# The begin of an eight-layer block on one NeuronCore: smaller first transfers, x and the first products taken piece by piece, and spare products ahead of both

## The chip, the cores and the metric

The kernel runs on one core of one Trainium2 chip. It is one launch that computes a whole eight-layer block for 256 tokens. The metric is the device time of that core in microseconds, lowest is best. Three runs of the kernel before took 2028.44, 2028.63 and 2031.82 us; their median, 2028.63 us, is the time before.

## The reference, cut to what matters

`x` has 256 tokens of 1024 features. Eight layers follow one another, each reading and adding to `x`: differential attention, a conformer convolution, latent attention, differential attention again, a window attention with a convolution, a gated feed-forward, a recurrent mixer and a mixture of eight experts. The change touches only what is computed first, the norm and the first projection of layer one:

```
def _rms_norm(x, g):
    xf = x.astype(jnp.float32)
    y = xf * lax.rsqrt(jnp.mean(xf * xf, axis=-1, keepdims=True) + NORM_EPS)
    return (y * g.astype(jnp.float32)).astype(x.dtype)

h = _rms_norm(x, a_norm_g[j])                       # (256, 1024)
proj = h @ w_in                                     # (1024, 4096): q, k, v, gate
q, k, v, gate = jnp.split(proj, [A_QK_WIDTH, 2 * A_QK_WIDTH, 2 * A_QK_WIDTH + A_WIDTH], axis=-1)
```

All later layers are computed by the same code in both kernels.

## The kernel before, in words

Tokens lie in two tiles of 128 partitions (`TILES`), features in eight chunks of 128 (`KC`). For a product TensorE needs the features on the partitions, so `norm_tensor` first turns `x`: 16 transposes of 128x128 (L1371), four to a PSUM bank, `("norm", 0, i)` for i from 0 to 3; each bank holds two chunks for both tiles. ScalarE (`high_parts`, L1105) and then VectorE (`low_parts`, L1117) read a bank, multiply by the norm's gain, which lies in the `vecs` part of the constants, and write `hT.high` and `hT.low`: every number is kept as two fp32r parts. `low_parts` frees the bank. The root of the mean square is left for later.

Weights come as granules of 128x2048 numbers (1 MB). A granule holds four chunks of 512 columns. The raw granule is split too: ScalarE writes `high`, VectorE writes `low` = raw - high. From the third granule on this is one instruction on each engine for a whole granule (L986, L989, called by `ahead`, which splits as many granules as there is room for before a given step). The first two are split in quarters of 128x512, one chunk each, by `split_first_piece` (L1000 on ScalarE, L1006 on VectorE). A product of one chunk is three matmuls of 512 columns (`three_passes`, L1022 to L1024): high by high, high by low, low by high. `products` takes granule 0, then granule 1: in each it goes through the four chunks for token tile 0 and then through the same four chunks for token tile 1. A granule is thus 2 x 4 x 3 = 24 matmuls.

SyncE issues every load, in the order of `sync_weights`: `x` tile 0, `x` tile 1, the first constants (`ident`, the identity that the transposes need, 16 columns for roots, and `vecs`: 656 columns, 328 KB), granule 0, the other constants (512 KB), `spread` (388 KB), granules 1 to 3, the lambdas and the router, then granules 4 and 5; from the seventh on a load waits until its buffer has been split. The constants have one semaphore, `const_landed`, for which TensorE, ScalarE, VectorE and GpSimd wait.

The order of the work on ScalarE at the begin is: load an activation table, the squares of tile 0, `hT.high` of banks 0 and 1, four quarters of granule 0, `hT.high` of banks 2 and 3, four quarters of granule 1, granule 2. VectorE does the same with the low parts; between granules 1 and 2 it computes twelve small tables for the rotation (`rope_tables`, L1046 to L1048).

Of the kernel before, what the change touches and what calls it, by code (L numbers as in the profile page):

```python
# [32 lines left out]
F32 = mybir.dt.float32  # L33
# [5 lines left out]
P = 128  # L39
# [635 lines left out]
class Core:  # L675


    def __init__(self, nc, ctx, w, consts, const_at, out, banks, plan):
# [40 lines left out]
        self.back, self.count, self.neghalf = const("back"), const("count"), const("neghalf")  # L719
        self.vecs = const("vecs").rearrange("p (c r) -> p c r", c=KC)  # L720
        self.first_const = const_at["cos"][0]


        at = 0
# [36 lines left out]

        self.x_landed = [sem(f"x_landed_{t}") for t in range(TILES)]
        self.const_landed = sem("const_landed")
        self.rest_landed = sem("rest_landed")
        self.spread_landed = sem("spread_landed")
        self.lambdas_landed = sem("lambdas_landed")
# [162 lines left out]

def sync_weights(k, sp):  # L930

    for t in range(TILES):
        sp.dma_start(k.x[:, t, :], k.w["x"][0].rearrange("(t p) d -> p t d", p=P)[:, t, :]).then_inc(k.x_landed[t], 16)
    sp.dma_start(k.const[:, 0:k.first_const], k.consts[:, 0:k.first_const]).then_inc(k.const_landed, 16)
    for g, granule in enumerate(k.granules):
        if g == 1:
            sp.dma_start(k.const[:, k.first_const:], k.consts[:, k.first_const:]).then_inc(k.rest_landed, 16)
            sp.dma_start(k.spread[:, :], k.w["spread"][:, 0:N_SPREAD].broadcast_to([P, N_SPREAD])).then_inc(k.spread_landed, 16)
        if g == 4:
            last_loads(k, sp)  # L940
        if g >= RAW:

            before = k.granules[g - RAW]
            if before.plain:
                k.wait_used(sp, before.last)
            else:
                sp.wait_ge(k.low_ready, before.number + 1)
        c, n = granule.shape
        sp.dma_start(k.raw[:, g % RAW, 0:c * n], k.w["weights"][g][:, 0:c * n]).then_inc(k.landed[g % RAW], 16)


def ahead(k, eng, name, limit=None):
# [36 lines left out]
        eng.tensor_tensor(low, raw, high.bitcast(F32), ALU.subtract).then_inc(k.low_ready, 1)  # L989


def split_first_piece(k, eng, g):

    n = GRANULE // 4
    if eng is k.nc.scalar:
        k.wait_landed(eng, g)
    for c in range(4):
# [16 lines left out]
def granule_parts(k, g, c):  # L1014

    n, slot = k.granules[g].shape[1], k.granules[g].number % SPLIT
    parts = Parts(k.high[:, slot, 0:c * n], k.low[:, slot, 0:c * n])
    return parts.rearrange("p (c n) -> p c n", c=c)


def three_passes(pe, out, lhs, rhs, start, stop):
# [226 lines left out]
def norm_scalar(k, act, n, x_from):  # L1248
    if n in RAW_NORMS:
        half_squares(k, act, x_from[0][0], 1)  # L1250
        high_parts(k, act, n, (2, 3))
        if n not in UNSCALED:
            act.wait_ge(k.rstd_ready, untiled(n) + 1)
            act.activation(k.h[:, 0, :], k.x[:, 0, :], ACT.Copy, scale=k.rstd[:, 0:1]).then_inc(k.h_ready, 1)
        ahead(k, act, ("norm", n, 3))
        return
    if n == 0:
        act.wait_ge(k.x_landed[0], 16)
        act.activation(k.h[:, 0, :], k.x[:, 0, :], ACT.Square, scale=float(D) ** -0.5, accum_out=k.ms[:, 0:1]).then_inc(k.ms_ready, 1)
        act.wait_ge(k.const_landed, 16)  # L1260
        high_parts(k, act, n, (0, 1))
        split_first_piece(k, act, 0)
        high_parts(k, act, n, (2, 3))
        split_first_piece(k, act, 1)
        ahead(k, act, ("norm", n, 3))
        return
    tiled_scalar(k, act, n, x_from)
    gain = NORM_GAIN[n]
    for i in range(4):
        name = ("norm", n, i)  # L1270
        if n == 1 and i % 2 == 0:
# [12 lines left out]

def norm_vector(k, v, n, x_from):
    if n in RAW_NORMS:
# [5 lines left out]
        ahead(k, v, ("norm", n, 3))  # L1292
        return
    if n == 0:
        v.wait_ge(k.x_landed[1], 16)
        v.tensor_tensor_reduce(k.h[:, 1, :], k.x[:, 1, :], k.x[:, 1, :], 1.0 / D, 0.0, ALU.mult, ALU.add, k.ms[:, 1:2])\
         .then_inc(k.ms_ready, 1)
        v.wait_ge(k.const_landed, 16)
        low_parts(k, v, n, (0, 1))
        split_first_piece(k, v, 0)  # L1300
        low_parts(k, v, n, (2, 3))
        split_first_piece(k, v, 1)
        b = a_buffers(k, 0)
# [5 lines left out]
        ahead(k, v, ("norm", n, 3))  # L1309
        return  # L1310
    tiled_vector(k, v, n, x_from)
    gain = NORM_GAIN[n]
# [42 lines left out]
def norm_tensor(k, pe, n):  # L1355
    k.normed, k.to_turn = (n, 0), None
    if n in RAW_NORMS:
        k.to_turn = n
        return
    if n in TILED:  # L1360
        tiled_tensor(k, pe, n)
        return
    pe.wait_ge(k.const_landed, 16)
    for t in range(TILES):
        pe.wait_ge(k.x_landed[t], 16)
    for i in range(4):
        k.take(pe, ("norm", n, i))
        for c in (2 * i, 2 * i + 1):
            for t in range(TILES):
                first = SEQ * (c % 2) + P * t  # L1370
                last = pe.transpose(k.bank(("norm", n, i))[:, first:first + P], k.x[:, t, P * c:P * (c + 1)], k.ident)  # L1371
        k.fill(last, ("norm", n, i))

def wait_normed(k, pe, parts):

# [8 lines left out]
def products(k, pe, names, g, lhs, kc, n, first=0, halves=2, ready=None, turn=None):  # L1384

    for half in range(halves):
        if g + half > 1:
            wait_split(k, pe, g + half)
        chunks = kc // halves
# [22 lines left out]
        if half < halves - 1:  # L1412
            last.then_inc(k.half_done, 1)
            if turn is not None:
                turn_x(k, pe, turn, (0, 1))


def channel_product(k, pe, name, g):
# [2312 lines left out]
def build(nc, w, consts, const_at, out, banks, plan, layers=LAYERS):  # L3731
    with ExitStack() as ctx:
# [44 lines left out]
        def _(pool):  # L3777
            k.engine_steps["pool"] = Steps(pool, k.own["pool"])
            for n, layer in enumerate(layers):
                if n == 0:  # L3780
                    for first, end, value in ((0, CHUNK, MASKED), (CHUNK, P, 0.0), (P, 2 * P, 1.0)):
                        pool.memset(k.late_keys[0:1, first:end].bitcast(F32), value).then_inc(k.late_keys_ready, 1)
                    pool.wait_ge(k.const_landed, 16)
                norm_pool(k, pool, n)
                if layer[0] == "a":
                    a_pool(k, pool, int(layer[1]))
# [73 lines left out]
```

## Time and profile before

| | us |
|---|---|
| median of three runs | 2028.63 |
| lowest and highest | 2028.44, 2031.82 |
| span of the profiled execution | 2030.7 |
| TensorE busy in it | 1940.3 |
| VectorE busy | 1566.0 |
| ScalarE busy | 1241.0 |
| GpSimd busy | 160.4 |

The profile is of one execution. Its span, from the first to the last instruction, is 2030.7 us; it gives no other time of its own, and this span is 2.1 us above the median of the runs shown and within their spread. All positions are microseconds from the start of the span. The 40 slices of the page show TensorE at nine tenths or more in 32 of them; the first slice, 51 us long, is at eight. The same page gives a mean of 249 GB/s for the DMA engines; the first slice has 330 GB/s.

### The profile page before, as it was taken

The numbers are of one execution on the slowest core, as the hardware profiler recorded it, in microseconds if no ns is written. First come the engines' busy times: TensorE is split into PE (matmuls) and PEld (weight loads), VectorE is DVE, ScalarE is ACT, GpSimd is POOL, SyncE is SP. The second block draws the span as 40 slices with busy tenths as digits, with TensorE's granted clock in tenths as the row PEclk, the third lists the DMA queues.
The fourth block names the chain that finished last, engine by engine and source line by source line (L and its number), as shares of the span: only waits on it lengthen the run. The fifth ranks groups of instructions, "written<-read, shape, count | busy, mean of one in ns | idle before, by whom it ended". The sixth has DMA issues, their size and how long they took to land.

```text
span 2030.7 us, 26201 instructions
## 1 busy us (share of the span) xinstructions
PE 1940.3 (96%) x9320; PEld 1619.0 (80%) x9320; DVE 1566.0 (77%) x1881; ACT 1241.0 (61%) x1461; POOL 160.4 (8%) x228
## 2 busy tenths in 40 slices
PE   8989988899989899999999999999999999999998
PEld 6867877778778788888878878888888888888886
DVE  7765966867656654446878898989889898998987
ACT  5562145645654544344767767777777777777775
POOL 4113401313011000000000000000000000000000
PEclk9999999999989999999999999999999999999999
DMA  8422234324324255553459999899999989999994
GB/s 330 157 84 104 93 125 140 125 104 180 113 82 178 92 207 187 187 187 125 187 229 382 355 353 376 343 382 351 372 375 349 376 342 385 353 373 374 341 376 174
DMA packets 71802, 504.78 MB, mean 249 GB/s; under 512 B 8864, under 2 KB 8864, under 8 KB 11808
## 3 DMA queue, kind: packets, MB, share of 16 engines
q1 hardware_dynamic: 70432, 498.87, 64.8%
q0 software_dynamic: 1280, 4.72, 0.6%
q8 instruction: 55, 0.90, 0.2%
q14 instruction: 35, 0.29, 0.0%
HBM read 501.46 MB, written 2.10 MB: 248 GB/s over the span
## 4 chain that ended last, share of the span: by engine, by line
PE 84%; DVE 8%; ACT 5%; issue 2%; POOL 1%; DMA 0%; DVEq 0%; SPq 0%; ACTq 0%; POOLq 0%
PE psum L1022 24%; PE psum L1024 24%; PE psum L1023 24%; PE psum L1958 4%; DVE low L989 3%; ACT high L986 2%; PE psum L3486 1%; PE psum L1966 1%; ACT h L1694 1%; PE psum L3417 0%; PE psum L1974 0%; DVE small L1738 0%; PE psum L1566 0%; DMA const<-in_constants 0%; PE psum L1143 0%
## 5 line engine op out<-in xcount | busy, mean ns | idle before, releaser
L989 DVE TENSOR_TENSOR low<-raw,high 128x2048 fp32r<-128x2048 f32 x459 | 1044.9, 2281 | 265.5 <-ACT high L986 261.9
L986 ACT ACTIVATE high<-raw 128x2048 fp32r<-128x2048 f32 x459 | 876.9, 1912 | 371.3 <-PE psum L1024 352.6
L1022 PE MATMUL psum<-high,yT_high 128*128 128x512 f32 (+1 forms) x1672 | 664.6, 397 | 25.9 <-DVE yT_low L3695 6.5
L1024 PE MATMUL psum<-high,yT_low 128*128 128x512 f32 (+1 forms) x1672 | 653.3, 391 | 0.0
L1023 PE MATMUL psum<-low,yT_high 128*128 128x512 f32 (+1 forms) x1672 | 652.1, 390 | 0.0
L1022 PEld LDWEIGHTS psum<-high,yT_high 128*128 128x128 f32 x1672 | 315.5, 189 | 95.6 <-issue 14.2
L1024 PEld LDWEIGHTS psum<-high,yT_low 128*128 128x128 f32 x1672 | 315.3, 189 | 67.1
L1023 PEld LDWEIGHTS psum<-low,yT_high 128*128 128x128 f32 x1672 | 316.0, 189 | 61.0
L1022 PE MATMUL psum<-high,hT_high 128*128 128x512 f32 (+2 forms) x560 | 220.8, 394 | 1.6 <-DVE low L1006 0.9
L1024 PE MATMUL psum<-high,hT_low 128*128 128x512 f32 (+2 forms) x560 | 217.3, 388 | 0.0
L1023 PE MATMUL psum<-low,hT_high 128*128 128x512 f32 (+2 forms) x560 | 217.3, 388 | 0.0
L1022 PEld LDWEIGHTS psum<-high,hT_high 128*128 128x128 f32 x560 | 106.0, 189 | 23.6 <-issue 1.8
L1024 PEld LDWEIGHTS psum<-high,hT_low 128*128 128x128 f32 x560 | 105.9, 189 | 21.5
L1023 PEld LDWEIGHTS psum<-low,hT_high 128*128 128x128 f32 x560 | 106.2, 190 | 20.1
L1958 PE MATMUL psum<-arena,raw 128*128 128x256 f32 x384 | 84.5, 381 | 0.0
L1958 PEld LDWEIGHTS psum<-arena,raw 128*128 128x128 f32 x384 | 73.4, 191 | 10.3 <-issue 0.2
L2065 DVE SCALAR_TENSOR_TENSOR arena<-arena,const 128x256 f32<-128x256 f32 x184 | 74.3, 480 | 0.4
L1022 PE MATMUL psum<-hT_high,high 128*128 128x256 f32 x224 | 66.9, 299 | 3.6 <-DVE hT_low L1325 2.4
L3343 POOL DMA_INDIRECT arena<-rows,index x7 | 8.7, 1242 | 765.1 <-DVE index L3692 765.1
L1023 PE MATMUL psum<-hT_low,high 128*128 128x256 f32 x224 | 65.8, 294 | 0.0
L1024 PE MATMUL psum<-hT_high,low 128*128 128x256 f32 x224 | 65.6, 293 | 0.0
L3550 ACT ACTIVATE arena<-psum 128x512 f32<-128x512 f32 x56 | 33.6, 599 | 45.6 <-PE psum L1024 45.6
(367 smaller groups left out, 1714.9 us busy)
## 6 DMA issues: line engine op xcount, KB each, us to landing
raw<-in_moe_weights SPq DMA_DIRECT2D x336, 1024.0 KB, 4.9
raw<-in_weights SPq DMA_DIRECT2D x132, 1024.0 KB, 4.9
raw<-in_weights SPq DMA_DIRECT2D x2, 896.0 KB, 4.7
raw<-in_weights SPq DMA_DIRECT2D x2, 768.0 KB, 8.1
x<-in_x SPq DMA_DIRECT2D x2, 512.0 KB, 3.9
raw<-in_weights SPq DMA_DIRECT2D x2, 512.0 KB, 3.6
rows<-h POOLq DMA_DIRECT2D x1, 1024.0 KB, 4.8
out_x<-x SPq DMA_DIRECT2D x1, 1024.0 KB, 5.5
```

The costliest lines, as they stand in the source:

```text
L986: eng.activation(high, raw, ACT.Copy).then_inc(k.high_ready, 1)
L989: eng.tensor_tensor(low, raw, high.bitcast(F32), ALU.subtract).then_inc(k.low_ready, 1)
L1022: pe.matmul(out, lhs.high, rhs.high, start=start, stop=False)
L1023: pe.matmul(out, lhs.high, rhs.low, start=False, stop=False)
L1024: return pe.matmul(out, lhs.low, rhs.high, start=False, stop=stop)
L1694: last = act.activation(probs[:, s % 2, SEQ * m:SEQ * m + e], k.bank(name)[:, SEQ * m:SEQ * m + e], ACT.Exp, bias=low[:, m:m + 1], scale=q ...
L1958: last = pe.matmul(k.bank(name)[:, SEQ * half:SEQ * (half + 1)], w[:, c, P * half:P * (half + 1)], b.hT[:, c, :], start=(c == 0), stop=(c ...
L1966: last = pe.matmul(k.bank(name)[:, SEQ * half:SEQ * (half + 1)], b.diagonals[i % 2][:, half, tap, :], b.padded[:, 2 * i + half, tap:tap + ...
L2065: last = v.scalar_tensor_tensor(b.conv[:, c, :], window, weight, b.conv[:, c, :], ALU.mult, ALU.add)
L3343: pool.indirect_dma_start(b.rows, None, rows, bass.IndirectOffsetOnAxis(ap=k.index[:, 0:1], axis=0)).then_inc(k.gathered, 16)
L3486: last = pe.transpose(k.bank(name)[:, P * c:P * (c + 1)], b.hidden[:, i % 2, P * c:P * (c + 1)], k.ident)
L3550: k.release(act.activation(b.silu[:, i % 2, :], k.bank(name), ACT.Silu), name)
```

## The change

The identity and 16 columns (144 columns, 72 KB) are loaded first, alone. Tile 1 of `x` follows on SyncE's queue; tile 0 is issued by ScalarE as its first instruction. `vecs` (256 KB) comes next with a semaphore of its own, then granule 0 as four transfers of 256 KB, one to a quarter, each with its semaphore. The other constants and `spread` move from ahead of granule 1 to behind granule 2. TensorE turns all of tile 0 and then all of tile 1. ScalarE and VectorE do one bank, two quarters, the next bank, two quarters. The products of granule 0 go chunk by chunk, both tiles in each, with both PSUM banks taken ahead. Twelve products of ones by ones (256 columns) are put ahead of the transposes and four ahead of the first real product; VectorE fills the ones first. The rotation tables move behind the split of granule 2.

```
+    sp.dma_start(k.const[:, 0:k.first_vecs], k.consts[:, 0:k.first_vecs]).then_inc(k.const_landed, 16)
+    load_x(k, sp, 1)
+    sp.dma_start(k.const[:, k.first_vecs:k.first_const], k.consts[:, k.first_vecs:k.first_const]).then_inc(k.vecs_landed, 16)
     for g, granule in enumerate(k.granules):
-        if g == 1:
+        if g == 0:
+            n = GRANULE // 4
+            for c in range(4):
+                cols = slice(n * c, n * (c + 1))
+                sp.dma_start(k.raw[:, 0, cols], k.w["weights"][0][:, cols]).then_inc(k.quarter_landed[c] if c < 3 else k.landed[0], 16)
+            continue
+        if g == 3:
             sp.dma_start(k.const[:, k.first_const:], k.consts[:, k.first_const:]).then_inc(k.rest_landed, 16)
             sp.dma_start(k.spread[:, :], k.w["spread"][:, 0:N_SPREAD].broadcast_to([P, N_SPREAD])).then_inc(k.spread_landed, 16)
...
+def load_x(k, eng, t):
+    eng.dma_start(k.x[:, t, :], k.w["x"][0].rearrange("(t p) d -> p t d", p=P)[:, t, :]).then_inc(k.x_landed[t], 16)
...
+def spare_products(k, pe, bank, n):
+    ones = k.yT.high[:, 0, :]
+    for _ in range(n):
+        pe.matmul(bank[:, 0:SEQ], ones[:, 0:P], ones, start=True, stop=True)
...
     if n == 0:                                     # norm_scalar
+        load_x(k, act, 0)
         act.wait_ge(k.x_landed[0], 16)
...
-        act.wait_ge(k.const_landed, 16)
-        high_parts(k, act, n, (0, 1))
-        split_first_piece(k, act, 0)
+        act.wait_ge(k.vecs_landed, 16)
+        for part in range(2):
+            high_parts(k, act, n, (part,))
+            split_first_piece(k, act, 0, (2 * part, 2 * part + 1))
...
+    pe.wait_ge(k.spare_ready, 1)                   # norm_tensor
+    k.take(pe, ("norm", n, 0))
+    spare_products(k, pe, k.bank(("norm", n, 0)), 12)
     pe.wait_ge(k.const_landed, 16)
     for t in range(TILES):
         pe.wait_ge(k.x_landed[t], 16)
-    for i in range(4):
-        k.take(pe, ("norm", n, i))
-        for c in (2 * i, 2 * i + 1):
-            for t in range(TILES):
+        for i in range(4):
+            if t == 0:
+                k.take(pe, ("norm", n, i))
+            for c in (2 * i, 2 * i + 1):
...
+def first_products(k, pe, names, lhs):
+    w = granule_parts(k, 0, 4)
+    for name in names:
+        k.take(pe, name)
+    spare_products(k, pe, k.bank(names[0]), 4)
+    for c in range(4):
+        wait_normed(k, pe, c // 2 + 1)
+        if c < 3:
+            pe.wait_ge(k.first_low, c + 1)
+        else:
+            wait_split(k, pe, 0)
+        for t, name in enumerate(names):
+            last = three_passes(pe, k.bank(name), lhs[:, c, P * t:P * (t + 1)], w[:, c, :], c == 0, False)
+    last.then_inc(k.half_done, 1)
```

`norm_vector` changes in the same way as `norm_scalar`, and its `ahead(k, v, ("norm", n, 3))` moves ahead of the two calls of `rope_tables`. GpSimd waits for `vecs_landed` as well.

TensorE at the begin of the program, before; `freed_0` and `freed_1` count how often VectorE has released PSUM banks 0 and 1, and `first_low` counts the low quarters:

```order
L1371 MATMUL psum<-const,x 128x128 [waits x_landed_1,x_landed_0,const_landed]
L1371 MATMUL psum<-const,x 128x128 x15
L1022 MATMUL psum<-high,hT_high 128x512 [waits first_low,freed_0]
L1023 MATMUL psum<-low,hT_high 128x512
L1024 MATMUL psum<-high,hT_low 128x512
L1022 MATMUL psum<-high,hT_high 128x512 [waits first_low]
```

And of the change:

```order
L1042 MATMUL psum<-yT_high 128x256 [waits spare_ready]
L1042 MATMUL psum<-yT_high 128x256 x11
L1402 MATMUL psum<-const,x 128x128 [waits x_landed_0,const_landed]
L1402 MATMUL psum<-const,x 128x128 x7
L1402 MATMUL psum<-const,x 128x128 [waits x_landed_1]
L1402 MATMUL psum<-const,x 128x128 x7
L1042 MATMUL psum<-yT_high 128x256 [waits freed_1,freed_0]
L1042 MATMUL psum<-yT_high 128x256 x3
L1046 MATMUL psum<-high,hT_high 128x512 [waits first_low,freed_0]
```

The transposes no longer wait for all of the constants, and half of them wait for one tile of `x` only; the four spare products ahead of the first real one wait for the release of bank 1 as well as bank 0.

VectorE up to the split of granule 1, before:

```order
L1296 ISA h,small<-x 128x1024 [waits x_landed_1]
L1296 ISA small 128x1
L1117 SCALAR_TENSOR_TENSOR hT_low<-psum,const,hT_high 128x256 [waits part_ready,const_landed]
L1117 SCALAR_TENSOR_TENSOR hT_low<-psum,const,hT_high 128x256
L1117 SCALAR_TENSOR_TENSOR hT_low<-psum,const,hT_high 128x256 [waits part_ready]
L1117 SCALAR_TENSOR_TENSOR hT_low<-psum,const,hT_high 128x256
L1006 TENSOR_TENSOR low<-raw,high 128x512 [waits first_high] x3
L1006 TENSOR_TENSOR low<-raw,high 128x512 [waits high_ready]
```

And of the change:

```order
L1321 MEMSET yT_high 128x256
L1323 ISA h,small<-x 128x1024 [waits x_landed_1]
L1323 ISA small 128x1
L1141 SCALAR_TENSOR_TENSOR hT_low<-psum,const,hT_high 128x256 [waits part_ready,vecs_landed]
L1141 SCALAR_TENSOR_TENSOR hT_low<-psum,const,hT_high 128x256
L1023 TENSOR_TENSOR low<-raw,high 128x512 [waits first_high] x2
L1141 SCALAR_TENSOR_TENSOR hT_low<-psum,const,hT_high 128x256 [waits part_ready]
L1141 SCALAR_TENSOR_TENSOR hT_low<-psum,const,hT_high 128x256
L1023 TENSOR_TENSOR low<-raw,high 128x512 [waits first_high]
L1023 TENSOR_TENSOR low<-raw,high 128x512 [waits high_ready]
```

Two quarters of granule 0 now stand ahead of the second pair of `hT_low`, whose last instruction is the one that releases bank 1.

SyncE's loads up to the fourth granule, of the change:

```order
L936 DMA const<-in_constants 128x144
L963 DMA x<-in_x 128x1024
L938 DMA const<-in_constants 128x512
L944 DMA raw<-in_weights 128x512 x4
L959 DMA raw<-in_weights 128x2048 x2
L947 DMA const<-in_constants 128x1024
L948 DMA spread<-in_spread 128x776
L959 DMA raw<-in_weights 128x2048
```

The loads ahead of the last quarter of granule 0 are of the same total size as those ahead of the end of granule 0 before; the two 512 KB and 388 KB loads stand two granules later.

## Rows read from the trace of the kernel before

**Rows 1.** The page's fourth part, shares of the chain that ended last.

```profile
PE 84%; DVE 8%; ACT 5%; issue 2%; POOL 1%; DMA 0%; DVEq 0%; SPq 0%; ACTq 0%; POOLq 0%
```

**Rows 2.** Chain of waits to 20 us, its longest pieces: start, us, what.

```profile
1.64 6.81 DMA const<-in_constants
8.49 1.13 PE psum L1371 x4
9.71 0.85 ACT hT_high L1105 x2
10.68 1.66 DVE hT_low L1117 x4
12.34 0.61 DVE low L1006
```

**Rows 3.** Stretch: us, PE, PEld, DVE, ACT, POOL busy, PEclk, DMA share, GB/s.

```profile
20.00:60.00 40.00, 40.00 (x187) 33.27 (x186) 34.47 (x50) 22.73 (x23) 17.75 (x12) 1.00 0.67 264
```

**Rows 4.** Timeline of TensorE: start, us, line, tile, [idle before].

```profile
8.49 3.68 PE L1371 MATMUL psum<-const,x 128*128 128x128 f32 x16 [8.49 <-DMA const<-in_constants]
13.08 0.77 PE L1022 MATMUL psum<-high,hT_high 128*128 128x512 f32 x1 [0.91 <-DVE low L1006]
...
17.48 0.45 PE L1023 MATMUL psum<-low,hT_high 128*128 128x512 f32 x1
17.77 0.40 PE L1024 MATMUL psum<-high,hT_low 128*128 128x512 f32 x1
18.00 0.40 PE L1022 MATMUL psum<-high,hT_high 128*128 128x512 f32 x1
```

**Rows 5.** Busy time by stretch of the begin, with the DMA columns.

```profile
1.70:5.50 3.80, 0.00 (x0) 0.00 (x0) 0.00 (x0) 1.45 (x3) 0.00 (x0) 1.00 0.95 317
5.50:8.50 3.00, 0.01 (x1) 0.01 (x1) 1.23 (x2) 0.00 (x0) 0.00 (x0) 1.00 1.03 359
8.50:13.00 4.50, 3.67 (x16) 3.27 (x16) 2.32 (x6) 3.29 (x8) 2.20 (x5) 1.00 1.01 362
```

**Rows 6.** Tile x up to 3 us: its two loads.

```profile
DMA to landing us min/median/max: 3.5/3.9/4.3
```

**Rows 7.** DMA packets from 6.6 to 8.0 us.

```profile
DMA packets 58, 0.48 MB, mean 339 GB/s; under 512 B 0, under 2 KB 0, under 8 KB 0
```

**Rows 8.** Timeline of ScalarE.

```profile
0.71 1.28 ACT L1259 ACT_TABLE_LOAD   x1 [0.71 <-PEq L3835]
...
9.71 1.63 ACT L1105 ACTIVATE hT_high<-psum,const 128x256 fp32r<-128x256 f32 x4 [4.31 <-PE psum L1371]
11.23 2.18 ACT L1000 ACTIVATE high<-raw 128x512 fp32r<-128x512 f32 x4
...
21.67 1.92 ACT L986 ACTIVATE high<-raw 128x2048 fp32r<-128x2048 f32 x1 [0.75 <-DMA raw<-in_weights]
```

**Rows 9.** Timeline of VectorE.

```profile
12.25 2.49 DVE L1006 TENSOR_TENSOR low<-raw,high 128x512 fp32r<-128x512 f32 x4
...
23.70 2.29 DVE L989 TENSOR_TENSOR low<-raw,high 128x2048 fp32r<-128x2048 f32 x1 [0.44 <-ACT high L986]
25.90 0.68 DVE L1852 TENSOR_TENSOR h<-psum,h 128x512 f32<-128x512 f32 x1
```

**Rows 10.** VectorE's groups by shape: a memset of 128x512.

```profile
L2370 DVE MEMSET arena<- 128x512 f32 x1 | 0.5, 485 | 0.1
```

**Rows 11.** Timeline of TensorE near 291 us.

```profile
290.82 0.77 PE L1022 MATMUL psum<-high,yT_high 128*128 128x512 f32 x1 [4.87 <-DVE yT_low L2108]
...
293.94 0.46 PE L1023 MATMUL psum<-low,yT_high 128*128 128x512 f32 x1
```

**Rows 12.** Busy time by stretch around it.

```profile
290.70:294.10 3.40, 3.28 (x8) 2.63 (x9) 1.74 (x5) 2.23 (x6) 0.00 (x0) 0.50 0.00 0
```

**Rows 13.** Timeline of TensorE near 596 us: products of 256 columns.

```profile
596.33 0.41 PE L1024 MATMUL psum<-hT_high,low 128*128 128x256 f32 x1
596.54 0.41 PE L1022 MATMUL psum<-hT_high,high 128*128 128x256 f32 x1
```

More of the change, by code:

```diff
@@ L721, in __init__ @@
         self.first_const = const_at["cos"][0]
+        self.first_vecs = const_at["vecs"][0]
         at = 0
@@ L763, in __init__ @@
         self.const_landed = sem("const_landed")
+        self.vecs_landed = sem("vecs_landed")
+        self.quarter_landed = [sem(f"quarter_landed_{i}") for i in range(3)]
+        self.spare_ready = sem("spare_ready")
         self.rest_landed = sem("rest_landed")
@@ L930, in sync_weights @@
 def sync_weights(k, sp):
-    for t in range(TILES):
-        sp.dma_start(k.x[:, t, :], k.w["x"][0].rearrange("(t p) d -> p t d", p=P)[:, t, :]).then_inc(k.x_landed[t], 16)
-    sp.dma_start(k.const[:, 0:k.first_const], k.consts[:, 0:k.first_const]).then_inc(k.const_landed, 16)
+    sp.dma_start(k.const[:, 0:k.first_vecs], k.consts[:, 0:k.first_vecs]).then_inc(k.const_landed, 16)
+    load_x(k, sp, 1)
+    sp.dma_start(k.const[:, k.first_vecs:k.first_const], k.consts[:, k.first_vecs:k.first_const]).then_inc(k.vecs_landed, 16)
     for g, granule in enumerate(k.granules):
-        if g == 1:
+        if g == 0:
[5 more added lines that the diff above has]
+        if g == 3:
             sp.dma_start(k.const[:, k.first_const:], k.consts[:, k.first_const:]).then_inc(k.rest_landed, 16)
@@ L989, in split, with split_first_piece @@
         eng.tensor_tensor(low, raw, high.bitcast(F32), ALU.subtract).then_inc(k.low_ready, 1)
-def split_first_piece(k, eng, g):
+def split_first_piece(k, eng, g, quarters=range(4)):
     n = GRANULE // 4
-    if eng is k.nc.scalar:
-        k.wait_landed(eng, g)
-    for c in range(4):
+    for c in quarters:
+        if eng is k.nc.scalar:
+            if g == 0 and c < 3:
+                eng.wait_ge(k.quarter_landed[c], 16)
+            elif g == 0 or c == 0:
+                k.wait_landed(eng, g)
         high, low, raw = (a[:, g, n * c:n * (c + 1)] for a in (k.high, k.low, k.raw))
@@ L1294, in norm_vector @@
     if n == 0:
+        v.memset(k.yT.high[:, 0, :].bitcast(F32), 1.0).then_inc(k.spare_ready, 1)
         v.wait_ge(k.x_landed[1], 16)
@@ L1297, in norm_vector @@
          .then_inc(k.ms_ready, 1)
-        v.wait_ge(k.const_landed, 16)
-        low_parts(k, v, n, (0, 1))
-        split_first_piece(k, v, 0)
+        v.wait_ge(k.vecs_landed, 16)
+        for part in range(2):
+            low_parts(k, v, n, (part,))
+            split_first_piece(k, v, 0, (2 * part, 2 * part + 1))
         low_parts(k, v, n, (2, 3))
         split_first_piece(k, v, 1)
+        ahead(k, v, ("norm", n, 3))
         b = a_buffers(k, 0)
@@ L1308, in norm_vector @@
         rope_tables(k, v, None, b.k_tables, k.wide("a_k_norm_g", 0, A_QK))
-        ahead(k, v, ("norm", n, 3))
         return
@@ L1365, in norm_tensor @@
         pe.wait_ge(k.x_landed[t], 16)
-    for i in range(4):
-        k.take(pe, ("norm", n, i))
-        for c in (2 * i, 2 * i + 1):
-            for t in range(TILES):
+        for i in range(4):
+            if t == 0:
+                k.take(pe, ("norm", n, i))
+            for c in (2 * i, 2 * i + 1):
                 first = SEQ * (c % 2) + P * t
                 last = pe.transpose(k.bank(("norm", n, i))[:, first:first + P], k.x[:, t, P * c:P * (c + 1)], k.ident)
-        k.fill(last, ("norm", n, i))
+            if t == 1:
+                k.fill(last, ("norm", n, i))
 def wait_normed(k, pe, parts):
@@ L1386, in products @@
     for half in range(halves):
+        if g + half == 0:
+            first_products(k, pe, names, lhs)
+            continue
         if g + half > 1:
@@ L3783, in _ @@
                     pool.wait_ge(k.const_landed, 16)
+                    pool.wait_ge(k.vecs_landed, 16)
                 norm_pool(k, pool, n)
```

## The prediction

> **What bounds the kernel now.** I read the shares of the chain first. TensorE has 84% of it and DMA rounds to 0% [rows 1]: what the begin takes from TensorE is all that this change can give. The chain in order of time then shows who holds the begin [rows 2]: the first constants are in flight from 1.64 to 8.45, then follow four transposes, two `hT_high` on ScalarE, four `hT_low` on VectorE, the first `low` quarter, and the first real product starts at 13.08 [rows 4]. The reader is to see that each link waits for the one ahead, so that a microsecond taken from the transfer is one taken from the first product, until something else comes last. Next I looked whether a gain would last. From 20 to 60 us TensorE is busy for 40.00 of 40.00 us while VectorE has 34.47 and ScalarE 22.73 [rows 3]: TensorE is the bound there and the two others have room, so an earlier start moves all later work with it.
>
> The timeline of TensorE shows a second cost. From 13.08 to 17.48 the products start 10 in 4.40 us, 0.43 each after the first; from 17.77 to 18.00 it is 0.23 [rows 4]. The clock column says 1.00 for this stretch [rows 5], but 0.43 is the spacing of a stretch whose granted clock is 0.50 (eight products in 3.4 us, [rows 11, 12]). So TensorE begins at its lower level of 1.2 GHz and goes to 2.4 GHz after 4.4 us of products. That costs 10 x 0.2 = 2.0 us.
>
> **The transfers.** In MB to a landing: identity 0.07, x 1.05, `vecs` 0.26, together 1.39; x with all first constants was the same 1.39. The engines are at 0.95 to 1.03 of their time and move 317 GB/s up to 5.5 us, then 359 and 362 [rows 5]; they are the limit, and the change removes no byte ahead of the end of granule 0. Tile 0 of x landed 3.5 us after its issue at 0.71, at 4.2, tile 1 at about 5.5 (4.3 after 1.17) [rows 6]. With the identity ahead and both tiles under way together I put tile 0 at 4.3 to 5.0 and tile 1 at 5.5 + 0.07/0.36 = 5.7. `vecs` would by bytes end 0.26/0.36 = 0.7 later, at 6.4. But before, the same 1.39 MB had landed only at 8.45, and no packet under 8 KB (the constants' are 2.6 KB) started between 6.6 and 8.0 [rows 7]: all but the last packets were through by about 6.9 and one late one held the landing. Without that `vecs` is there by 6.9, with it at 8.5. I take 6.9, nearer to the packet rows, and keep 8.5 as an end. The quarters follow at 0.73 us each: 7.6, 8.3, 9.0, 9.8; granule 1 is 2.9 later, 12.7, granule 2 at 15.6.
>
> The row says that the sixteen engines were already full with one queue. The Trainium skill says in "DMA: Bandwidth & Descriptors", section "Issuing engines are not separate DMA queues", that loads issued by several engines run on the same 16 DMA engines and only the issue time is saved; the trace agrees in its 0.95 share. If the second queue doubled the rate, both tiles would be there at 3.7 and the first product another 0.6 us earlier.
>
> **The first product, step by step.** The ones (128x256) take VectorE half of 485 ns [rows 10] from 0.7 on. Twelve spare products at 0.21 (the spacing of 256 columns at the lower level, [rows 13]) run from 1.1 to 3.7, ahead of tile 0: cost 0. They would cost if x came at 3.7 or before. ScalarE's issue (0.4) and its table load (1.28, [rows 8]) end at 2.4, also under the transfer. Transposes are 3.68/16 = 0.23 apart [rows 4]: tile 0 from 4.3 to 6.15, tile 1 from the later of that and 5.7, so bank 0 is filled with the second transpose of tile 1, at 6.15 + 2 x 0.23 and about 0.3 of latency, 6.9. That is when `vecs` is there; ScalarE starts at 7.0.
>
> ScalarE: `hT_high` is 1.63/4 = 0.41, a quarter 2.18/4 = 0.55 [rows 8]. Bank 0 done at 7.85, quarters 0 and 1 at 8.95, bank 1 at 9.8, quarters 2 and 3 at 10.9. VectorE: `hT_low` 0.41 [rows 2], a low quarter 2.49/4 = 0.62 [rows 9]. It starts 0.1 behind ScalarE, as at 10.68 before: bank 0 from 8.0 to 8.8, quarters 0 and 1 to 10.05, bank 1 to 10.9, quarters 2 and 3 to 12.15.
>
> Now the wait that the change adds. The four spare products need bank 0 and bank 1, and behind them stands every real product. Bank 1 is released at 10.9, though bank 0 and quarter 0 are ready at 9.4. So 1.5 us of the quicker first chunk are not used. The spare ones run from 11.0 to 11.85 (4 x 0.21), and the first real product starts at 11.85, against 13.08: 1.23 us. The chunk order then asks for a quarter every six products (2.6 us) where before it was every three; quarters 2 and 3 at 11.5 and 12.15 are in time. The halves of granule 1 are low from about 14.5 to 16.5, wanted at 19.
>
> The clock: TensorE is busy without a gap from 11.0. It rose 4.4 us after the first product in one place and 3.1 us (290.82 to 293.94, after 4.87 idle, [rows 11]) in the other. I take 4.4: it rises at 15.4. Real products at the lower level are (15.4 - 11.85)/0.43 = 8.3 in place of 10.3, a gain of 2 x 0.2 = 0.4. With 3.1 it is 5.3 of them, a gain of 1.0. That the transposes or the twelve spare ones help is not in the sum: before, 16 transposes in a row from 8.49 to 12.17 did not spare the products 4.4 us of the lower level. The Trainium skill says the same in "TensorE: Matmul & The Clock Gate", "Part 4: PE-mode transpose": such transposes don't count as TensorE being busy for its clock. By that rule the gap between 3.7 and 11.0 is idle to the gate and the twelve are lost; the sum goes by this. If transposes counted, the clock would be up by 11, which is the first rival.
>
> **Later effects, each at nothing.** The other constants and `spread` now follow granule 2: 15.6 + 0.92/0.36 = 18.2. The tables come after the low part of granule 2 (about 18 to 20.3), so at 20.3 to 21.7; their first user ran at 25.90, behind granule 3's low part (23.70 + 2.29, [rows 9]), which hangs on the landing of granule 3 at 21.67 [rows 8]. Bytes ahead of that are the same, so this user does not come earlier, nor later. TensorE needs granule 3 at about 30 and the freed bank 0 after that: cover of 4 us. If it is gone, each us late costs one. GpSimd's wait for `vecs` ends earlier than its wait for the constants did.
>
> Sum: 1.23 + 0.4 = 1.6 us less. The profiled span of 2030.7 would be 2029.1. That span is 2.1 above the median; the difference is taken off both sides, so 2028.6 - 1.6 = 2027.0.
>
> **The rivals.**
>
> A. The clock is up at the first real product. For it: twelve spare ones, 16 transposes and four spare ones are 2.6 + 3.7 + 0.9 us of work in the ten ahead. Against: the idle time between, and the 4.4 us after the transposes before. Then the four spare ones take 0.45, the first product starts at 11.45, and none is slow: 1.63 + 10.3 x 0.2 = 3.7 less, 2024.9. Chance 0.15.
>
> B. The late packet comes again, in `vecs`. Everything behind moves by 1.5: first product at 13.35, 0.27 later than before; the clock, counted from the spare ones at 12.5, rises at 16.9 and 8.3 products are slow: 0.4 back. Result 0.1 less, 2028.5. Chance 0.2.
>
> C. Slower: more stretches at half clock later on. The stretch at 290.7 cost 8 x 0.2 = 1.6 us after a gap of 4.87 us. All such gaps stay as long as they are but now lie 1.6 us earlier, and whether the clock falls in one is not fixed: the three runs of one kernel are 3.4 us apart, two such stretches. One more than before takes back the gain; from the second on the kernel is slower: 2027.0 + 3.3 = 2030.3. For it: that spread. Against: as many could be lost as won. Chance 0.1.
>
> D. The start does what I say but the cover is gone: VectorE's later tables or the transfers hold TensorE before 60 us and the whole is 2028.6. Against it: the room in [rows 3]. Chance 0.05.
>
> My own case has 0.5, with 2026.4 to 2027.8 as its own range (clock up after 3.1 us; `vecs` at 7.7). The range must reach A on one side and part of C on the other: 2024.0 to 2029.6. About 0.2% of the time, 4.1 us, is what a measurement of this kernel tells from no change. Only A with luck at a later gap, or my case with two half-clock stretches fewer, is beyond it: 0.1. Slower by as much needs C with three or more: 0.03. Within it: 0.87.
>
> **What would show it.** In the changed profile: twelve 256-column products up to 3.7; first transpose at 4.3 to 5.0; `hT_high` at 7.0; the four spare ones directly after the fourth `hT_low`, near 11.0, with bank 1 as what they waited for; the first product of 512 columns near 11.85; spacing of 0.43 until 15.4; TensorE without a gap from there to 60 us. I am wrong if the spacing is 0.23 at the first product (A), if `hT_high` waits for `vecs` past 8 (B), or if TensorE shows gaps up to 60 us (D). Counting half-clock rows in both tells C.

## The result and the profile after

| | kernel before | kernel changed |
|---|---|---|
| median, us | 2028.05 (20 runs) | 2031.47 (20 runs) |
| mean and its standard error | 2027.89 ± 0.51 (18 runs) | 2031.02 ± 0.39 (19 runs) |
| profiled execution: span | 2030.7 | 2028.0 (time 2029.85) |

Two of the 20 runs of before (2446.51 and 2788.13 us) and one of the change (3255.97 us) were slow ones: the medians are over all 20, the means and the ratio over the others. The ratio is 1.0014 with the interval 1.0008 to 1.0021: the change makes the kernel 1.6 to 4.3 us slower, 3.1 by the means. It was forecast to be 1.6 us faster. The two profiled executions stand the other way round, so two spans say nothing here on the sign.

The chain of waits of the changed kernel (start, length, what):

```profile
1.64 0.42 SPq L938
2.11 6.87 DMA raw<-in_weights
9.00 0.63 ACT high L1017
...
10.28 0.73 ACT hT_high L1129 x2
11.04 0.89 DVE hT_low L1141 x2
12.06 1.19 PE psum L1042 x4
13.25 0.43 PE psum L1046
```

Where a transfer of constants led to the transposes [rows 2], the first quarter of the weights now leads to bank 1's `hT_low`, and that to the four spare products. The timeline of TensorE in the changed kernel:

```profile
1.17 2.93 PE L1042 MATMUL psum<-yT_high 128*128 128x256 f32 x12 [1.17 <-DVE yT_high L1321]
4.96 3.65 PE L1402 MATMUL psum<-const,x 128*128 128x128 f32 x16 [0.86 <-DMA x<-in_x]
12.06 1.19 PE L1042 MATMUL psum<-yT_high 128*128 128x256 f32 x4 [3.45 <-DVE hT_low L1141]
13.05 0.63 PE L1046 MATMUL psum<-high,hT_high 128*128 128x512 f32 x1
...
17.32 0.45 PE L1047 MATMUL psum<-low,hT_high 128*128 128x512 f32 x1
17.61 0.40 PE L1048 MATMUL psum<-high,hT_low 128*128 128x512 f32 x1
```

The transposes stand 3.5 us earlier than in [rows 4], yet the first real product starts at 13.05 against 13.08, behind 3.45 us without work and the four spare products. Ten products are 0.43 apart, then the spacing falls to 0.23, as it did before. The rows of ScalarE show that it waits for the weights and takes bank 1 (`hT_high`, at 10.19) only behind two quarters; two rows of VectorE follow:

```profile
7.43 0.84 ACT L1129 ACTIVATE hT_high<-psum,const 128x256 fp32r<-128x256 f32 x2 [1.43 <-PE psum L1402]
9.00 1.28 ACT L1017 ACTIVATE high<-raw 128x512 fp32r<-128x512 f32 x2 [0.73 <-DMA raw<-in_weights]
10.19 0.82 ACT L1129 ACTIVATE hT_high<-psum,const 128x256 fp32r<-128x256 f32 x2
...
9.67 1.34 DVE L1023 TENSOR_TENSOR low<-raw,high 128x512 fp32r<-128x512 f32 x2 [0.39 <-ACT high L1017]
11.04 0.88 DVE L1141 SCALAR_TENSOR_TENSOR hT_low<-psum,const,hT_high 128x256 fp32r<-128x256 f32 x2
```

Busy time by stretch (PE, PEld, DVE, ACT, POOL, clock, DMA share, GB/s), to hold against [rows 5] and [rows 3]:

```profile
5.50:8.50 3.00, 3.00 (x15) 2.71 (x13) 1.33 (x3) 1.35 (x4) 0.69 (x3) 1.00 0.99 297
20.00:60.00 40.00, 40.00 (x186) 33.31 (x185) 32.84 (x52) 21.83 (x22) 17.87 (x12) 1.00 0.66 263
```

The 16 DMA engines are as full as before and move 297 GB/s where they moved 359. TensorE has no gap from 20 to 60 us in either kernel.

### The profile page after: what moved, and what is told of

It is laid out like the page before. It is cut to its first block, busy times and chain, and to the rows that moved or that the text cites. A ratio compares the mean times of both kernels' runs of the same rounds, so it can differ in the third digit from the quotient of the medians.

```text
span 2028.0 us, 26239 instructions
## 1 busy us (share of the span) xinstructions
PE 1941.1 (96%) x9336; PEld 1620.3 (80%) x9336; DVE 1566.5 (77%) x1882; ACT 1242.2 (61%) x1461; POOL 160.5 (8%) x228
## 4 chain that ended last, share of the span: by engine, by line
PE 84%; DVE 8%; ACT 5%; issue 2%; POOL 1%; DMA 0%; SPq 0%; DVEq 0%; ACTq 0%; POOLq 0%
PE psum L1046 24%; PE psum L1048 24%; PE psum L1047 24%; PE psum L2010 4%; DVE low L1003 3%; ACT high L1000 2%; PE psum L3538 1%; PE psum L2018 1%; ACT h L1746 1%; PE psum L3469 0%; PE psum L2026 0%; DVE small L1790 0%; PE psum L1618 0%; DMA raw<-in_weights 0%; PE psum L1167 0%
```

## The experiments

Below, "the 25th" is the start of the 25th product of 512 columns, the first of granule 1: it holds both the later start and the slow products. A slow product is one whose successor starts 0.43 behind it, not 0.23. In the first trace of before the 25th is at 20.76, in that of the change at 20.60. Means have their standard error; that of a difference of two means is 0.4 to 0.7, so kernels less than about 1 us apart are not told apart by their means. The means of before in the three sessions are 2027.90 (e1 to e4), 2027.44 (e5 to e8) and 2027.40 (e9 to e12); "above before" is the difference to the one beside. The change is 3.1 above before.

**e1: the kernel before again.** Is its first trace a usual one? No edit.

> The kernel before once more, for its own profile, for the clock and span of every run and for what a ratio of two equal kernels is. Theory M (the profiled execution of before was a late one: its first constants hung on one late packet): here the constants land near 7 instead of 8.45, the first 512-column product starts near 11.5 instead of 13.08, so that the change never had 1.2 us to win. Rival N (before always starts its products near 13.1, and the change loses elsewhere): start at 12.9 to 13.2 again. Theory O (the time outside the span is longer in the change): time minus span here is 1.1 to 1.2 us in every run, against 1.8 to 1.9 for the change. Ratio 0.999 to 1.001.

Timeline of TensorE:

```profile
6.55 3.51 PE L1371 MATMUL psum<-const,x 128*128 128x128 f32 x16 [6.55 <-DMA const<-in_constants]
11.13 0.47 PE L1022 MATMUL psum<-high,hT_high 128*128 128x512 f32 x1 [1.07 <-DVE low L1006]
11.44 0.40 PE L1023 MATMUL psum<-low,hT_high 128*128 128x512 f32 x1
```

The constants landed at 6.50, not 8.45 [rows 2]; the first product is 1.95 earlier, and from it on the spacing is 0.23: no slow product. The 25th is at 16.67, four microseconds ahead of the first trace. The time was 2028.76 ± 0.61, ratio 1.0005 (0.9995 to 1.0015): the same kernel, 0.9 above itself.

**e2 and e3: one part of the change undone.** All of `x` on SyncE; no spare products.

```
e2:  sync_weights:  + load_x(k, sp, 0)       norm_scalar:  - load_x(k, act, 0)
e3:  - spare_products(k, pe, k.bank(("norm", n, 0)), 12)
     - spare_products(k, pe, k.bank(names[0]), 4)
```

> The changed kernel with tile 0 of x loaded by SyncE, behind the identity, as all other loads; ScalarE issues no load. Theory O (ScalarE's own load, the first use of its queue, costs 0.7 us outside the span): time minus span falls from 1.85 to 1.15, tile 0 lands a little later (one more issue, 0.4 us) but tile 1 not, and the time falls by 0.4 to 0.7 us against the change, ratio to before near 1.0010. Rival: the longer time outside comes from more semaphores or code; then time minus span stays at 1.85 and the ratio at 1.0014.

> The changed kernel without its 16 spare products and without the fill of ones. Theory P (they do nothing for the clock and the last four only stand in the way): first real product 0.85 us earlier, directly after bank 1 is released at about 12.0; the spacing goes from 0.43 to 0.23 within 3 to 5 us of it; time 0.4 us less than the change (0.85 earlier, 0.4 given back as slow products). Rival Q (they bring the clock up earlier in many executions): time 0.5 to 1.5 us more than the change.

e2: ratio 1.0016 (1.0008 to 1.0025), mean 2031.22 ± 0.49, 3.3 above before; `x` landed at 4.87 and 6.15 against 4.83 and 6.13. The second queue gives nothing and costs nothing. Time less span was 1.81 to 1.82 for before and 1.86 to 1.88 for the change, so no cost hides outside the span either. e3: 1.0010 (1.0001 to 1.0018), mean 2030.36 ± 0.50, 2.5 above before, the 25th at 19.46. Without spare products TensorE waits 3.77 and starts at 12.31:

```profile
12.31 0.49 PE L1046 MATMUL psum<-high,hT_high 128*128 128x512 f32 x1 [3.77 <-DVE hT_low L1141]
12.62 0.61 PE L1047 MATMUL psum<-low,hT_high 128*128 128x512 f32 x1
```

The second product follows 0.31 behind the first, the later ones 0.43: the clock was up and fell 0.3 us after the start. So the four spare products delay the first real one by 0.7 and bring no clock; the 0.7 between the means of e3 and the change is within their error.

**e4 and e5: bank 1 asked for late; then also one load for granule 0.**

```
-    for name in names:
-        k.take(pe, name)
+    k.take(pe, names[0])
...
+            if c == 0 and t == 1:
+                k.take(pe, name)
e5 also:
+            sp.dma_start(k.raw[:, 0, :], k.w["weights"][0][:, :]).then_inc(k.landed[0], 16)
```

> The changed kernel, but bank 1 is asked for only ahead of the first product of tile 1; the spare four and the first three products need bank 0 alone. Theory R (the wait for both banks holds every product for 1.5 us or more): the spare four start at 10.4 and the first real product at 11.3 in place of 13.05; it then waits for bank 1 at 12.0 once; the end of granule 0 comes 0.7 to 1.2 us earlier and so does the time. Rival: the clock rises at a fixed place later on and the three products gained are slow ones; then 0.3 to 0.5 us.

> The kernel e4 (bank 1 asked for late) with granule 0 loaded in one transfer of rows of 8 KB, as before the change, instead of four of rows of 2 KB. Theory S (the four transfers are slower, not just cut): granule 0 lands at 9.0 to 9.3 as a whole, as in the kernel before, against 11.0 to 11.3 with quarters, granule 1 at 11.7 against 13.7; the DMA rate from 6 to 8 us is 400 GB/s and not 190 to 270. ScalarE's first quarter starts at 9.1 in place of 9.3, so the time is 0.2 to 0.4 us less than e4. Rival (the rate falls there for another reason, such as VectorE and ScalarE reading at that time): granule 0 lands at 11 again and ScalarE's first quarter starts there, the time is 2 us more.

Timeline of TensorE in e4:

```profile
4.91 2.30 PE L1402 MATMUL psum<-const,x 128*128 128x128 f32 x16 [0.81 <-DMA x<-in_x]
8.63 0.74 PE L1042 MATMUL psum<-yT_high 128*128 128x256 f32 x4 [1.43 <-DVE hT_low L1141]
10.81 0.47 PE L1046 MATMUL psum<-high,hT_high 128*128 128x512 f32 x1 [1.44 <-DVE low L1023]
...
12.27 0.79 PE L1046 MATMUL psum<-high,hT_high 128*128 128x512 f32 x1 [0.35 <-DVE hT_low L1141]
```

The first product is 2.2 earlier and the mean falls to 2028.14 ± 0.41, 0.2 above before (ratio to before 1.0000, 0.9992 to 1.0009). Without the wait for both banks nearly the whole loss is gone. Here the clock was up for the first two products and fell in the third. Stretches by DMA, e4 first, then e5:

```profile
6.00:8.00 2.00, 1.09 (x8) 0.85 (x8) 1.53 (x3) 0.84 (x2) 0.38 (x2) 1.00 0.99 227
```

```profile
6.00:8.00 2.00, 1.09 (x8) 0.86 (x8) 1.53 (x3) 0.84 (x2) 0.39 (x2) 1.00 1.07 446
```

In quarters the transfers move at half the rate in this stretch. In all nine traces with quarters it is 207 to 291 GB/s there (the change 252); in the eight with one load it is 383 to 446, but for the first trace of before (328); in two halves (e12) it is 230. Small packets by themselves are not the price. From 8 to 9 us, 216 of the changed kernel's 219 packets are under 8 KB as well, and the engines move 414 GB/s:

```profile
8.00:9.00 1.00, 0.61 (x3) 0.21 (x1) 0.60 (x2) 0.28 (x1) 0.83 (x3) 1.00 1.07 414
```

The landings of its quarters are 0.65 to 0.67 apart, too. What makes the two microseconds before that slow is not shown. As one load (e5) all of granule 0 is there at 9.22 instead of 11.27. But that is when the first quarter came anyway, and the first product starts at 10.75 against 10.81: mean 2028.16 ± 0.45, 0.7 above before, nothing gained.

**e6: e4, and the gap filled with twelve more spare products.**

```
+    spare_products(k, pe, k.psum[:, 4, :], 12)      # behind the transposes
```

> The kernel e4 with twelve more spare products directly behind the transposes, into PSUM bank 4, which nobody else uses yet, so they wait for nothing. Theory T (what the change loses beside the late start is the clock, which is lost in the idle time between transposes and products): the clock, once up during the transposes, stays up, the first real product starts at 10.8 to 11.1 as in e4 and the spacing is 0.23 from there in most executions; the 25th product starts at 16.5 to 17.2 in place of 18.3; mean time 1.0 to 1.5 us less than e4. Rival (the spare products don't count for the clock): spacing 0.43 again for 3 to 4 us and the time of e4.

```profile
8.40 2.34 PE L1042 MATMUL psum<-yT_high 128*128 128x256 f32 x16
10.58 0.40 PE L1046 MATMUL psum<-high,hT_high 128*128 128x512 f32 x1
```

TensorE's timeline has no slow product and its 25th is at 16.80, as in e1 (16.67). The mean is 2027.84 ± 0.22, 0.4 above before, ratio 1.0003 (0.9994 to 1.0012): as before, not better. Expected was 1.0 to 1.5 less than e4, which the mean does not show. It is also the steadiest of all: its runs have a standard deviation of 0.74 us.

**e7 and e8: parts on their own.** e7 is before with the identity first and `x` turned by tile; e8 is the change with before's order on ScalarE and VectorE.

```
e7:  + sp.dma_start(k.const[:, 0:k.first_vecs], ...)      # ahead of x
     - for i in range(4): ... for t in range(TILES):
     + for t in range(TILES): ... for i in range(4):
e8:  + high_parts(k, act, n, (0, 1))
     + split_first_piece(k, act, 0)                       # the same for low parts
```

> The kernel before with the identity loaded first, the rest of the first constants behind x, and the transposes by tile; no spare products, granule 0 in one transfer, all on SyncE, order of the other work as before. Theory T: the transposes start at 4.9 instead of 6.5 but the first product hardly earlier (10.8 against 11.1), since ScalarE and the weights follow; the gap of TensorE grows from 1.1 to 2.5 us and in part of the executions the clock falls in it: time within 0.5 us of before on either side. Rival U (earlier transposes are a gain that the other parts of the change hide): 0.5 to 1.5 us less than before.

> The changed kernel, both banks still asked for ahead of the spare products, but ScalarE and VectorE do banks 0 and 1 and then the four quarters, as before the change. Theory R (the late release of bank 1, behind two quarters, is the loss): ScalarE does bank 1 at 8.3 while it would wait for quarter 0, bank 1 is released at about 10.1 instead of 11.9, the spare four start there and the first real product at 10.7 to 11.0; time 2 to 3 us less than the change, as e4. Rival: it is the spare products and the chunk order themselves; then the time stays within 0.7 us of the change.

Timeline of TensorE in e7:

```profile
5.45 3.61 PE L1374 MATMUL psum<-const,x 128*128 128x128 f32 x16 [5.45 <-DMA x<-in_x]
11.29 0.47 PE L1025 MATMUL psum<-high,hT_high 128*128 128x512 f32 x1 [2.22 <-DVE low L1009]
...
12.29 0.59 PE L1026 MATMUL psum<-low,hT_high 128*128 128x512 f32 x1
12.68 0.63 PE L1027 MATMUL psum<-high,hT_low 128*128 128x512 f32 x1
```

Turning `x` 1.1 us earlier than e1 does not start the products earlier (granule 0 landed at 9.75, in e1 at 9.01), but it widens the gap to 2.22, and the clock falls at 12.3. Mean 2027.85 ± 0.39, 0.4 above before. e8 has the four spare ones at 10.20 instead of 12.06 and its first product at 11.19: 2028.17 ± 0.29, 0.7 above before. With bank 1 early again, asking for both banks costs nothing that the mean shows.

**e9: the change with only its gap filled.** Twenty spare products behind the transposes; the wait for both banks stays.

> The changed kernel as it is, both banks asked for ahead, with 20 more spare products directly behind the transposes into PSUM bank 4, so that TensorE is idle for 1 us or less where it was idle for 3.4. It separates the clock from the late start. Theory T: the first real product stays at 12.5 to 13.1, the spacing is 0.23 from there, the 25th product starts at 18.0 to 18.5 against 20.6, 19.7 and 19.5 in the three traces of the change and its near copies; mean time 1.3 to 2.3 us less than the change (2031.0), spread of the runs smaller. Rival: the clock comes up as late as ever; time as the change.

```profile
8.24 3.48 PE L1042 MATMUL psum<-yT_high 128*128 128x256 f32 x20
11.94 0.71 PE L1042 MATMUL psum<-yT_high 128*128 128x256 f32 x4 [0.21 <-DVE hT_low L1141]
12.49 0.39 PE L1046 MATMUL psum<-high,hT_high 128*128 128x512 f32 x1
```

The first product is only 0.56 earlier than in the change, but none is slow, and the 25th is at 17.95. The mean falls to 2027.72 ± 0.47, 0.3 above before, ratio 1.0000 (0.9991 to 1.0009). So keeping the clock up is worth as much as the earlier start in e4: curing either takes back the loss, and in the means the two do not add up (e6, with both, is at 0.4 with its 25th 1.15 ahead of that of e9; the error is 0.4 to 0.6).

**e10 to e12: the loss put into before, and two tries at a better kernel.** e10 has the change's order on both engines and asks for both banks; e11 is before with 28 spare products ahead of the transposes and 14 behind; e12 is e7 with granule 0 in two halves and 16 and 14 spare ones.

```
e10: +        if g + half == 0:
     +            for name in names: k.take(pe, name)
e11: +    spare_products(k, pe, k.psum[:, 4, :], 28)
     +    spare_products(k, pe, k.psum[:, 4, :], 14)
e12: +            sp.dma_start(k.raw[:, 0, 0:n], k.w["weights"][0][:, 0:n]).then_inc(k.first_half, 16)
```

> The kernel before with one part of the change alone: ScalarE and VectorE do bank 0, two quarters, bank 1, two quarters, and TensorE asks for both banks ahead of its first product. Loads, transposes and the order of the products as before, no spare products. Theory R: the first product waits for bank 1, released at 12.0, and starts at 12.1 instead of 11.1; TensorE is idle for 2.0 us ahead of it instead of 1.1; mean time 1 to 2 us more than before. Rival (the part is harmless by itself): time within 0.5 us of before.

> The kernel before with nothing but spare products: 28 of them from 1.2 us on, ahead of the transposes, and 14 behind the transposes, all into PSUM bank 4. Theory T: the clock is up when the constants land at 6.5, the transposes take 1.8 us instead of 3.5, ScalarE starts hT_high at 7.1, granule 0 at 9.1 as it lands, the first real product starts at 10.3 to 10.5 with a spacing of 0.23 in all executions; mean time 1 to 2 us less than before. Rival (the transfers alone set the begin): first product at 11.1, time 0 to 0.5 us less.

> A version that puts together what helped: identity first, both tiles of x, then the gains, all on SyncE; granule 0 in two transfers of rows of 4 KB; transposes by tile; the old order of banks and quarters on ScalarE and VectorE; 16 spare products ahead of and 14 behind the transposes into bank 4. By the transfers the first half of granule 0 lands at 8.1 and the first real product starts at 9.8 to 10.3 at a spacing of 0.23; the 25th starts at 15.4 to 16.0 against 16.7 in the better trace of before; mean time 1 to 2 us less than before. Rival (rows of 4 KB are slow as those of 2 KB were, or the transposes hold the begin): first product at 10.8 or later and the time of before.

Timelines of TensorE, e11 and then e12:

```profile
6.86 1.91 PE L1382 MATMUL psum<-const,x 128*128 128x128 f32 x16
8.52 1.92 PE L1026 MATMUL psum<-yT_high 128*128 128x256 f32 x14
10.92 0.47 PE L1030 MATMUL psum<-high,hT_high 128*128 128x512 f32 x1 [0.48 <-DVE low L1007]
```

```profile
6.90 1.92 PE L1038 MATMUL psum<-yT_high 128*128 128x256 f32 x14
11.10 0.47 PE L1042 MATMUL psum<-high,hT_high 128*128 128x512 f32 x1 [2.28 <-DVE low L1019]
...
12.42 0.63 PE L1044 MATMUL psum<-high,hT_low 128*128 128x512 f32 x1
```

e10: first product at 12.27 behind 1.76 of idle, slow, the 25th at 19.48, 2.5 later than before usually has it. Expected was 1 to 2 us slower; measured 2027.82 ± 0.36 against 2027.40, ratio 1.0003 (0.9994 to 1.0012). The trace shows the loss and the times hardly do. The granted clocks of the runs explain part of it: their mean is 0.9905 over the 11 runs of e10, the highest of all kernels, against 0.9898 for before. Over the 256 runs of this kernel and its versions whose span and clock are on record, 0.001 of mean clock goes with 1.1 us less span (a straight line fitted within each version and session). An estimate from this line: at the same clock e10 is 1.1 ± 0.4 above before, in the expected range. Why its clock is higher stays open. e11: 1.0002 (0.9993 to 1.0011); there was no slow product to save, and the first product is only 0.5 earlier (10.92 against 11.44). e12: 0.9999 (0.9990 to 1.0008); its half of granule 0 landed at 9.57, not 8.1, and the gap of 2.28 loses the clock. Both were expected to be 1 to 2 us faster. No version beats before by what can be measured.

**e13 to e16: two more traces of each kernel.**

> The kernel before, a third trace. Theory M: the constants land at 6.4 to 7.0 and the first product starts at 11.1 to 11.6, as in the second trace, not at 13.08 as in the first. The 25th product starts at 16.5 to 17.0 where the clock is up at the first product and at 18.0 to 19.2 where it is not. Rival N: the late constants are the rule, first product near 13.

> The kernel before, a fourth trace, with the same expectations as the third: first product at 11.1 to 11.6 (M) or near 13 (N).

> The changed kernel, a second trace. Theory: first real product at 12.8 to 13.1 again, after 3.4 us of idle TensorE, at a spacing of 0.43; the 25th product at 19.3 to 20.8, so 2 to 4 us behind the better traces of before. Rival (its first trace was a bad one too): first product near 12.0 and the 25th at 17.5 or earlier.

> The changed kernel, a third trace, with the same expectations as the second: 25th product at 19.3 to 20.8, or by the rival at 17.5 or earlier.

TensorE in e13 and e15 (e14 starts its products at 11.80, e16 at 13.28):

```profile
6.80 3.68 PE L1371 MATMUL psum<-const,x 128*128 128x128 f32 x16 [6.80 <-DMA const<-in_constants]
11.39 0.47 PE L1022 MATMUL psum<-high,hT_high 128*128 128x512 f32 x1 [0.91 <-DVE low L1006]
11.70 0.39 PE L1023 MATMUL psum<-low,hT_high 128*128 128x512 f32 x1
```

```profile
12.29 1.20 PE L1042 MATMUL psum<-yT_high 128*128 128x256 f32 x4 [3.79 <-DVE hT_low L1141]
13.29 0.63 PE L1046 MATMUL psum<-high,hT_high 128*128 128x512 f32 x1
```

The 25th is at 16.67, 16.91 and 17.34 in the three later traces of before, mean 16.97, and at 20.60, 20.29 and 20.54 in the three of the change, mean 20.48. The begin thus loses 3.5 us: the first product 1.8 later (11.44 to 13.21), and 8 to 10 slow products at 0.2 more. With the first trace of before counted in, the mean of before is 17.92 and the loss 2.6. The measured loss is 3.1. By the same line as for e10 the change is 2.5 ± 0.3 above before at equal clock (e9: 0.0 ± 0.4), and its lower mean clock (0.9890 over 19 runs, 0.9898 over the 101 of before in the three sessions) adds about 0.9. That is one stretch of 3.4 us at half clock more in an execution. Such a stretch is recorded at the begin of e2 and e3, of the changed kernel's three traces in none, so it isn't shown whether it lies there or later. Span and mean clock of e15 and e16:

```profile
core 0: 2026.7 us, clock 0.992
```

```profile
core 0: 2030.3 us, clock 0.988
```

Two executions of the same kernel with the same begin are 3.6 us apart, and what differs is the half-clock stretches further on (30.7 and 41.0 us of them between 20 and 2,000 us; 41.0 in all four traces of before, 34.1 in the change's first). That is why a single span could mislead.

## Why the prediction was wrong

**The base.** "The first real product starts at 13.08" was true of one execution. The prediction saw that one packet had held the constants until 8.45 and gave the changed kernel a transfer without it, at 6.9, but kept the packet in the kernel it compared with. Three of four traces are without it: first product 11.13 to 11.80. With 11.44 as base the predicted 11.85 would have been 0.4 later, not 1.23 earlier. This alone takes the forecast gain of 1.6 to nothing (0.4 lost, 0.4 won), and it is the step that failed first; the next one turns the sign.

**"It rises at 15.4", 4.4 us after the first product in both.** In those three traces of before there is no slow product at all: 16 transposes of 3.3 to 3.7 us and only 0.9 to 1.3 us of idle time stand ahead. So "a gain of 0.4" was a loss of 1.7 to 2. ([rows 5], named for the clock column of this stretch, end at 13.00; the row that shows its 1.00 stands in the last section.) The sum also went by the Trainium skill's "TensorE: Matmul & The Clock Gate", "Part 4: PE-mode transpose", that transposes don't count. These traces disagree: e1, e13 and e14 have nothing but transposes on TensorE ahead of the products, and these run 0.23 apart at once. In e14 the last three transposes start 0.11 apart, the others 0.21: there the clock rose while TensorE did nothing but transposes. The row the prediction rested on [rows 4] had the same 3.68 us of transposes and 0.91 of idle and was slow; 3 of 4 executions are not. What separates it from e13, with the same two lengths, no trace shows. Another section of the Trainium skill's page, "Part 1: The HAM clock gate (the "warmup" mystery)", says that one and the same kernel can have different numbers of slow products in different runs. These traces agree, with ten and none; the prediction gave before's number no spread.

**The gap.** "TensorE is busy without a gap from 11.0" held from 12.06, but the idle stretch ahead was taken as already paid for. It is what the change adds: the transposes end 3.5 us earlier and what follows them does not start earlier, 3.45 of idle for 0.91. In e9, with the gap filled, no product is slow and the loss is 0.3 in place of 3.1.

**The wait for both banks** was in the prediction, with bank 1 released behind two quarters, at 10.9. The mechanism was right; its cost was read as 1.5 us "not used" of a gain. It came at 11.9, since quarter 0 landed at 8.98, not at 7.6, and e4 and e8 put its removal at 2.9 and 2.4 (3.1 less what they are above before).

**The quarters** "at 0.73 us each" held between themselves (0.65 to 0.67), but the first came 2.2 behind `vecs` (8.98), not 0.7 (7.6), and so the last at 10.97 and not at 9.8: from 6 to 8 us the engines moved 252 GB/s, where the sum had 360. With one load (e5) the first product was no earlier once bank 1 was asked for late.

**Right were:** the second queue (no gain, e2), `vecs` (6.77 for 6.9), `x` tile 0 (4.83 in 4.3 to 5.0; tile 1 6.13 for 5.7), the twelve spare ones at no cost, ScalarE's bank 0 (7.43 for 7.0), and no gap to 60 us, so that D fell. A's premise, that the clock can be up at the first product, holds for before and not for the change (e2 and e3 keep it for 0.3 us). B needed its late packet in `vecs`; it was in before. C's price was seen between executions (e15, e16). Between the kernels the three traces and the runs disagree: 35.3 us of half clock on average against 41.0 in the traces, yet a lower mean clock in the runs of the change, about 0.9 us. So C may have a part in the loss, but not most of it. The range did not fit C either: its own time, 2030.3, lies above the upper end of 2029.6, beyond which only 0.03 was left.

## What to carry over

Read the begin of a kernel in three or four executions before a term of 2 us is taken from it, and give both kernels the same luck in a transfer. Work that is moved earlier only widens a gap unless what waits behind it moves too; on TensorE the gap can cost the clock as well as the time. Take a buffer where it is first needed, not with its neighbours: ask which work of the releasing engine now stands ahead of the release.

## What the hardware showed

- The same idle length has no fixed price. After 0.9 to 1.3 us the clock was up in three traces and not in one. After 1.4 (e4, e5) and 2.2 to 2.3 (e7, e12) it was up at the first product and fell 0.5 to 1.1 us later, while TensorE was working; after 1.59 (e8) and 1.76 (e10) it was down. After 3.4 to 3.8 it was down in the three traces of the change, and in e2 and e3 it was up and fell 0.3 us later.
- The clock column can say 1.00 while the spacing tells 1.2 GHz, in the first trace of before, where ten products start 0.43 apart [rows 4]; in e2 it does say 0.50. Spacing is the safer reading. Busy time by stretch, before and then e2:

```profile
13.00:17.50 4.50, 4.42 (x11) 3.48 (x12) 3.62 (x8) 2.85 (x7) 2.75 (x1) 1.00 1.01 424
12.40:15.80 3.40, 3.40 (x11) 2.76 (x10) 3.40 (x8) 3.29 (x8) 0.37 (x1) 0.50 1.00 418
```

- Behind the same twelve spare products the clock was up from the first transpose in e4 and e5 (16 in 2.3 us instead of 3.65) and for none of them in the change, e2, e6, e8 and e9. With 28 (e11) it was up from the first, with 16 (e12) from the fourth on.
